# Six small loads on ScalarE's queue, moved from behind the plain products to the fifth Strassen unit

## Reference

```python
bcx = jnp.einsum('bsd,de->bse', x, w_in)              # layer one: 1024 -> 3 x 1024
gb, gc, xh = jnp.split(bcx, 3, axis=-1)
conv, new_buf = causal_dwconv(gc * xh, buf, conv_w)
y = jnp.einsum('bsc,cd->bsd', gb * conv, w_out)
...
xp = layer_norm(ALPHA * xp + yp, ln1_g[i], ln1_b[i])
mp = hier_moe(xp, moe_w_group[i], moe_w_expert[i], ...)  # 4 groups x 8 experts, top 2
xp = layer_norm(ALPHA * xp + mp, ln2_g[i], ln2_b[i])
```

## Time and profile before

| | us |
|---|---|
| median of 3 executions | 1400.19 (1399.59 to 1404.52) |
| the profiled execution, its own time | 1400.29 |
| its span in the trace | 1398.5 |
| TensorE busy | 1339.6 (96% of the span) |
| VectorE, ScalarE, GpSimd busy | 542.7, 217.6, 122.6 |
| mean granted clock of TensorE | 0.995 of full |

### The profile page before, as it was taken

One profiled execution on the slowest core, in us unless ns is written; L12 is line 12 of the kernel. 1 busy time (PEld: TensorE's weight loads), 2 busy tenths in 40 slices (PEclk: granted clock), 3 DMA queues, 4 the chain that ended last, 5 costly groups with the idle time before them and its releaser, 6 DMA issues.

```text
span 1398.5 us, 20258 instructions
## 1 busy us (share of the span) xinstructions
PE 1339.6 (96%) x8660; PEld 892.2 (64%) x8660; DVE 542.7 (39%) x1157; ACT 217.6 (16%) x383; POOL 122.6 (9%) x138
## 2 busy tenths in 40 slices
PE   8899999999999999998899999999999999999896
PEld 7688876665555555665378888666555555566552
DVE  4667676322111211331346888652211111213217
ACT  0000014000000010100134444220000001010012
POOL 0000001101100110111010000010001100111100
PEclk9999999999999999999999999999999999999999
DMA  9800269999999999999993113799999999999995
GB/s 390 295 1 0 94 278 357 409 426 426 426 427 425 427 426 424 426 424 426 390 318 114 61 60 121 277 365 424 427 426 425 425 428 426 427 426 424 425 404 216
DMA packets 67587, 472.48 MB, mean 338 GB/s; under 512 B 16383, under 2 KB 26623, under 8 KB 39584
## 3 DMA queue, kind: packets, MB, share of 16 engines
q1 hardware_dynamic: 51485, 448.84, 77.3%
q0 software_dynamic: 11520, 15.52, 3.1%
q10 hardware_dynamic: 4490, 6.80, 1.5%
HBM read 468.38 MB, written 27.32 MB: 354 GB/s over the span
## 4 chain that ended last, share of the span: by engine, by line
PE 86%; DMA 9%; ACT 1%; ACTq 1%; DVE 1%; issue 1%; POOL 0%; SPq 0%; POOLq 0%
PE ps L1081 28%; PE ps L1117 15%; PE ps L727 9%; PE ps L773 9%; PE ps L817 7%; PE ps L1046 7%; DMA ring<-in_moe_w_down 3%; DMA ring<-in_moe_w_up 3%; PE ps L1034 3%; PE ps L1219 1%; DMA ring<-yrows 1%; ACTq L1290 1%; PE ps L1105 1%; PE ps L1057 1%; PE ps L834 1%; DMA yrows<-A,Bt 1%
## 5 line engine op out<-in xcount | busy, mean ns | idle before, releaser
L1081 PE MATMUL ps<-ring,A 128*64 128x256 f32 x4096 | 456.6, 380 | 16.5 <-DMA ring<-in_moe_w_up 8.1
L1081 PEld LDWEIGHTS ps<-ring,A 128*64 128x64 f32 x4096 | 325.3, 137 | 158.2 <-issue 39.4
L1117 PE MATMUL ps<-ring,A 128*64 128x512 f32 x1024 | 233.8, 597 | 7.1 <-issue 1.1
L2021 DVE TENSOR_TENSOR A<-A,ps 128x256 f32<-128x256 f32 x64 | 27.0, 421 | 542.0 <-PE ps L1081 542.0
L1117 PEld LDWEIGHTS ps<-ring,A 128*64 128x64 f32 x1024 | 76.0, 136 | 119.4 <-issue 112.7
L727 PE MATMUL ps<-A,ring 128*128 128x260 f32 x576 | 128.0, 383 | 0.3 <-DMA ring<-in_a_w_in 0.3
L727 PEld LDWEIGHTS ps<-A,ring 128*128 128x128 f32 x576 | 109.4, 190 | 17.4 <-DMA ring<-in_a_w_in 0.6
L662 POOL DMA_INDIRECT A<-x,idx x42 | 44.8, 1067 | 673.9 <-PE ps L1034 626.3
L1046 PE MATMUL ps<-C,Bt 104*64 104x512 f32 x400 | 95.6, 620 | 0.0
L2024 DVE COPY A<-ps 128x256 f32<-128x256 f32 x64 | 27.2, 425 | 121.1 <-PE ps L1105 121.1
L1434 ACT ACTIVATE A<-ps 128x512 f32<-128x512 f32 x42 | 25.1, 597 | 304.7 <-PE ps L1117 304.7
(11 more groups left out here) (295 smaller groups left out, 1154.9 us busy)
## 6 DMA issues: line engine op xcount, KB each, us to landing
ring<-in_moe_w_gate SPq DMA_DIRECT2D x62, 2048.0 KB, 24.2
ring<-in_moe_w_up SPq DMA_DIRECT2D x60, 2048.0 KB, 26.4
ring<-in_moe_w_down SPq DMA_DIRECT2D x60, 2048.0 KB, 27.5
ring<-yrows SPq DMA_DIRECT2D x10, 1024.0 KB, 11.1
ring<-in_a_w_in SPq DMA_DIRECT2D x6, 1536.0 KB, 27.1
ring<-in_moe_w_down SPq DMA_DIRECT2D x8, 1024.0 KB, 41.8
ring<-in_b_w_in SPq DMA_DIRECT2D x8, 1024.0 KB, 11.9
ring<-in_moe_w_up SPq DMA_DIRECT2D x6, 1024.0 KB, 43.1
```

What stands on the lines that cost most here:

```text
L1081: mm = pe.matmul(ps[hf * ROWS:(hf + 1) * ROWS, (GATE_BANK, 3)[u], :FH], xgT[:, k, :], ring[:, slot, col:col + FH], start=(k == 0), stop=(k ...
L1117: mm = pe.matmul(ps[nh * ROWS:(nh + 1) * ROWS, 2, :], hidT[:, at:at + ROWS], ring[:, slot, m * D + nh * 512:m * D + (nh + 1) * 512], start ...
L2021: tt(gated, gated, ps[:, 3, :FH], ALU.mult).then_inc(ready, 1)
```

## The change

The six loads are issued at another place of ScalarE's list: no longer behind the copy of the second plain product, but behind the copy of part 0 of the fifth unit (u = 4). The loads themselves, their number, sizes, semaphores and targets, the other lists and all waits stay as they are.

```diff
+SMALL_LOADS = 4
...
             for c in range(2):
                 act.wait_ge(mm_in[0], c + 1)
                 act.activation(halves(tmp[c]), banks(c), ACT.Copy).then_inc(ev_a[0], 1)
-                if c == 1:
-                    router_weights(act, 0)
-                    for l in L:
-                        for j, name in enumerate(("ln1_g", "ln1_b")):
-                            act.dma_start(gb[:, 2 * l + j, :], a[name][l].rearrange("(p k) -> p k", k=KT)
-                                          ).then_inc(gb_in, 16)
             for u in range(len(UNITS)):
                 act.wait_ge(mm_in[0], PLAIN + 7 * u + 1)
                 if u >= 2:
                     act.wait_ge(ev_b[0], 7 * (u - 1))
                 act.activation(tmp[5][:, (u % 2) * HALF:(u % 2 + 1) * HALF], ps[:, part_bank(u, 0), :HALF], ACT.Copy
                                ).then_inc(ev_a[0], 1)
+                if u == SMALL_LOADS:
+                    router_weights(act, 0)
+                    for l in L:
+                        for j, name in enumerate(("ln1_g", "ln1_b")):
+                            act.dma_start(gb[:, 2 * l + j, :], a[name][l].rearrange("(p k) -> p k", k=KT)
+                                          ).then_inc(gb_in, 16)
```

## The result

The changed kernel takes 1391.78 us (median of 6 executions, 1389.31 to 1395.66); the kernel before, on the same chip, 1400.33. The ratio is 0.9938, 95% interval 0.9919 to 0.9957: by the ratio 8.7 us less, between 6.0 and 11.3. 1392.0 was forecast.

What follows compares the result with a forecast made beforehand. TensorE's own work was taken as the bound (busy 96% of the span). Stall 6.47 plus slow restart 1.68 gave 8.15 us off, 1400.29 to 1392.1, so 1392.0 us for the median; range 1390.0 to 1396.5.

Steps and rivals of the forecast that it cites:

- The stall: TensorE's wait before part 1 of the second Strassen unit, behind ScalarE's late copy, would go: 6.47 us.
- The slow restart: Second to third unit's part 1 takes 13.95 us, not 12.27, the clock having fallen in the pause: 1.68 us.
- Why the issue took 16.30 us: ScalarE's issue of a 4 KB row waits for room on its queue, draining slowly behind SP's large transfers.
- What is late next: VectorE becomes last to arrive, with 5.5 us to spare at the first addition and 4.6 at weight_sums(2).
- The loads at their new place: At the fifth unit six issues hold ScalarE 3 to 8 us, upper bound 19.3; cost taken: 0.
- The cover of 23 us: How long ScalarE can be held at the fifth unit before TensorE waits: 97.2 - 73.2 less 1 us.
- Passed on to the end: Every stage behind the units follows TensorE's signal, so the 8.15 us gain reaches the end.
- The head start: Output projection and first expert load would begin at 157.0 and 157.4 us, 8.15 us earlier.
- the span of 1390.4: The span forecast for the profile after the change: 1390.4 us.
- one of the prediction's own signs of being wrong: The prediction is wrong if the head start of 8.15 us at 157 is smaller at the end.
- Case B: Stall goes, but part is given back in full-engine stages or elsewhere: 1393.2 to 1397 us, likeliest 1394; chance 0.18.
- Within or over 0.5%: Whole kernel: faster by over 0.5% (under 1393.2 us) 0.74, within 0.5% 0.23, slower by over 0.5% 0.03.

Runs made afterwards that it cites:

- experiment 4: The kernel before, loads in their old place, with part 0 of the second unit computed four times in TensorE's wait: 1398.18 us.
- experiments 2 and 3: Against the kernel before, only the four rows (2) or only the two router loads (3) moved to the fifth unit: 1392.32 and 1391.37 us.
- Experiments 1 and 5: Changed kernel with the six loads behind the first unit's copy instead (1), and there with the router loads issued twice (5): 1392.47 and 1402.37 us.
- experiment 6: The changed kernel run again without an edit, for a second profile: 1391.89 us, ratio 0.9932.
- experiment 9: Changed kernel with six spare products on TensorE ahead of its wait for layer one's first gather: 1393.99 us.
- 10: Changed kernel with 24 memsets ahead of layer one's first gather and 18 spare products in TensorE's wait: 1395.55 us.
- 8: Changed kernel with 24 memsets in GpSimd's list ahead of layer one's first gather: 1398.15 us.

## Why the prediction was right, point by point

**The stall (6.47 us), right.** Part 1 of the second unit was due at 35.82 and starts at 35.73; in that execution everything from the first unit on is 0.09 us earlier. From part 1 to part 1 it is 12.27 us. The cause is shown: with the issues gone from ahead of that copy (all six, the four rows or the two router loads) the stall is gone, and with the issues ahead of the next copy there is a hold and no stall.

**The slow restart (1.68 us), right.** In the changed kernel it is gone by the windows, and in experiment 4 by itself: 1.61 us. Together, part 1 of the third unit is 8.24 us earlier, of which 0.09 is the start; 8.15 was the sum.

**Why the issue took 16.30 us, right, with more to it.** It waits behind the router loads' rows on ScalarE's own queue; that is now shown by experiments 2 and 3 and not only argued. The full engines are the other half: in front of idle ones (share 0.00 in that stretch) the same six in the same order are issued in 0.39 to 0.60 us each. That it is SP's transfers which fill them follows from the packets (below); no run takes SP's transfers away alone, and none shows how much room the queue has. The rule of the Trainium skill's page "DMA: Bandwidth & Descriptors" ("Issuing engines are not separate DMA queues"), that the sequencer's time to initiate a transfer is usually small relative to the transfer, fits the six at their new place loosely (0.39 to 0.60 us, with 1.7 to 3.4 us to landing) and fails for the one that took 16.30 of its 25.5 us to landing.

**What is late next, right.** VectorE's first addition came at 29.62 and the sums of the third unit ended at 43.55, for 29.8 and 43.5 forecast.

**The loads at their new place, right.** ScalarE was held for 3.1 us, the low end of 3 to 8. The cover of 23 us rested on subtraction, and at the fifth unit no run tests it. Experiments 1 and 5 test the like cover at the first unit, which ends at about 48: held until 41.7 there was no stall, held until 55.5 there was one. I did not try its edge.

**Passed on to the end, right in the median, not in each execution.** The head start was 8.24 us at 157. It is there at the end in the medians (8.7 and 9.5 us, intervals 6.0 to 11.3 and 7.7 to 11.3), and in experiment 6's profile. With executions from 1389.31 to 1395.66, a median within 0.3 us of the forecast is in part luck. The first profile kept only 4.6 us of it: for that execution the span of 1390.4 was missed by 3.5 us, and one of the prediction's own signs of being wrong, a head start that is smaller at the end, is there. Case B is what that one shows: part lost to the clock falling at another place, priced at 1393.2 to 1397, likeliest 1394; it was 1395.66. But I had thought mainly of the rate of the full stages, and it is one wait of TensorE for a gather, which the trace before didn't have and the prediction didn't name. In the seven other profiles without an edit at that place the wait is 0 (before, 2, 3 and 6), 0.4 (1) and 0.7 to 0.8 us (4 and 5); in that of experiment 9 it would have been 2.0. It grows with the time at which the gather is issued, counted from part 1 of the third unit: no wait at 182.8 to 183.4 us (before, 2, 3 and 6), 0.4 at 183.8 (1), 0.7 and 2.0 at 184.1 (4 and the first profile). The same issue time with two different waits says that the landing differs too. I can't say from these runs that the changed kernel has that wait more often than the one before; its six later executions are within 1390.21 to 1392.35, experiments 2 and 3 have one each of 1397 and 1400, and the kernel before has some of its own of 1403 to 1407.

**Within or over 0.5%.** 0.62% and 0.68%, over the bound of 0.5% as forecast; the lower end of the first interval (0.43%) is under it, that of the second (0.55%) is not.

## What to carry to other kernels

Don't read an engine's busy share for the cost of its issues: look in the chain for a transfer whose issue is long, and ask which instruction stands behind it and when its result is wanted. Moving either the many-rowed loads or what follows them is enough, and the cheapest new place is behind a copy whose successor is wanted late. A pause of the matrix engine has a second price where its clock falls, so compare the same work before and after the pause, and check the stage that follows for waits that are now at the edge.

## What the runs showed of the hardware

- ScalarE's queue took 2048 short rows (two transfers) in 1 us with the DMA engines full (1.9 us in experiment 1), and then held the next transfer, be it 128 pieces or 1024. That hold ended at 39.4 to 40.1 us in four profiles (before, 4, 1 and 5), whether it had begun at 23.1, 23.7, 25.8 or 25.7: it depended on what the engines had worked off far more than on when the wait began. SP's queue holds its engine too: in the kernel before, SP's first write of zeros (L579) is in its issue for 23.80 us from 11.53 on, and the second for 3.95. In the kernel before, from 24 to 36 us, short rows and SP's packets of 11 KB went through nearly one for one, 396 to 453. From 40 to 50 us, when SP's packets had 2 KB, it was still nearly one for one, 1778 to 1566, and the short rows went at five times the pace (178 per us, after 33):

```profile
q1 hardware_dynamic: 453, 4.99, 99.2%
q10 hardware_dynamic: 396, 0.01, 1.9%
```

```profile
q1 hardware_dynamic: 1566, 3.15, 86.2%
q10 hardware_dynamic: 1778, 0.15, 13.4%
```

(q1 is SP's queue, q10 ScalarE's; packets, MB, share.) With the engines idle, at 73 us, the six loads landed in 1.7 to 3.4 us; before they needed 10.1 to 26.7.

- Spare or repeated products in a pause kept TensorE's clock at 1.00 where it had fallen without them: 12.34 us in place of 13.95 for the same 56 records (experiment 4), and 1.00 in place of 0.54 behind the wait for the late gather (10 against 8).

- Two waits of TensorE of nearly the same length, at the same place of the program, ended differently: 2.10 us with the clock at 1.00 behind it, and 2.00 us with 0.66 over 10 us. What decides between them, no run here shows.
